# Narrow products between wide ones in two stages, and products of constants in a third

## The reference

```
x = x + 0.5 * swiglu(rmsnorm(x), ffn1)               # ffn
p = rmsnorm(x) @ w_in                                # mixer with convolution and delta rule
    y_a = gelu(u_a) * spatial_gating(gelu(v_a))
    qkv = silu(causal_dwconv(qkv)); q, k l2-normed
    beta = sigmoid(b_raw); g = -exp(a_log) * softplus(a_raw + dt_bias)   # 4 + 4 narrow columns of w_in
    o = gated_delta_rule(q, k, v, beta, g)           # chunks of 64 tokens
x = x + concat(y_a, rmsnorm(o) * silu(z)) @ w_out
x = x + 0.5 * swiglu(rmsnorm(x), ffn2);  x = rmsnorm(x, final_norm)
h = rmsnorm(x); q, k, v, og, f_logit, u = split(h @ hy_w_in)             # f_logit: 8 narrow columns
    cum = cumsum(log_sigmoid(f_logit + f_bias))      # the forgetting mixer's decay
    attn = softmax(q k^T * scale + c_i - c_j, causal) @ v * sigmoid(og)
x = x + concat(attn, pooled(u)) @ hy_w_out
x = x + swiglu(...)
x = x + rwkv7_time_mix(rmsnorm(x))                   # bonus = sum(r * k * r_k) per head, times v
x = x + swiglu(...)
```

## Time and profile before

| | us |
|---|---|
| median of 3 runs (1346.1 to 1346.85) | 1346.11 |
| the profiled execution | 1346.0 |
| its span in the profile | 1344.2 |
| PE busy / POOL / ACT / DVE | 1290.8 / 752.5 / 597.8 / 545.2 |

### The profile page before, as it was taken

How to read it: one execution, slowest core, us unless ns; L and a number is a source line. 1 busy time by engine, 2 the same in 40 slices (tenths; PEclk the granted TensorE clock), 3 DMA queues, 4 the chain that set the end, 5 groups by cost and what they waited for, 6 DMA issues and landing times.

```text
span 1344.2 us, 22609 instructions
## 1 busy us (share of the span) xinstructions
PE 1290.8 (96%) x9424; PEld 1130.2 (84%) x9424; DVE 545.2 (41%) x798; ACT 597.8 (44%) x773; POOL 752.5 (56%) x190
## 2 busy tenths in 40 slices
PE   6999999999999999897999999989998998999999
PEld 5888888888888888797698888867887997988887
DVE  4433334634333333437333333365847434333333
ACT  6444443224454444634455444434232334544442
POOL 2988850112478888565248888800034321698885
PEclk9999998999999999988899999989989997999999
DMA  6655552234255555444124555513441011455552
GB/s 260 211 195 188 187 198 94 94 106 177 96 179 197 187 187 187 151 155 157 63 78 173 192 191 194 196 71 130 152 156 67 3 34 34 166 209 188 187 190 91
DMA packets 30570, 200.74 MB, mean 149 GB/s; under 512 B 3488, under 2 KB 5408, under 8 KB 6688
## 3 DMA queue, kind: packets, MB, share of 16 engines
q1 hardware_dynamic: 27632, 195.39, 40.8%
q10 hardware_dynamic: 2864, 4.27, 1.0%
HBM read 197.55 MB, written 2.10 MB: 149 GB/s over the span
## 4 chain that ended last, share of the span: by engine, by line
PE 90%; DVE 5%; ACT 3%; issue 1%; DMA 0%; POOL 0%; SPq 0%; ACTq 0%; DVEq 0%
PE psum L326 24%; PE psum L328 12%; PE psum L317 9%; PE psum L319 8%; PE psum L318 8%; PE psum L911 7%; PE psum L922 5%; PE psum L2333 1%; PE psum L2425 1%; DVE arena L1709 1%; PE psum L2441 1%; PE psum L314 1%; PE psum L1801 1%; PE psum L1800 1%; PE psum L2455 1%
## 5 line engine op out<-in xcount | busy, mean ns | idle before, releaser
L2742 POOL TENSOR_TENSOR wlo<-raw,whi 128x2048 fp32r<-128x2048 f32 x154 | 714.1, 4641 | 458.9 <-ACT whi L287 439.4
L326 PE MATMUL psum<-f_both,whi 128*128 128x512 f32 x1408 | 493.7, 394 | 2.1 <-DVE arena L835 2.1
L287 ACT ACTIVATE whi<-raw 128x2048 fp32r<-128x2048 f32 x154 | 294.9, 1916 | 254.9 <-PE psum L328 171.0
L328 PE MATMUL psum<-f_both,wlo 128*128 128x256 f32 x1408 | 394.3, 280 | 0.0
L326 PEld LDWEIGHTS psum<-f_both,whi 128*128 128x128 f32 x1408 | 265.2, 188 | 61.3 <-issue 2.7
L328 PEld LDWEIGHTS psum<-f_both,wlo 128*128 128x128 f32 x1408 | 265.4, 189 | 1.5
L317 PE MATMUL psum<-whi,ahi 128*128 128x512 f32 x352 | 137.3, 390 | 0.0
L319 PE MATMUL psum<-whi,alo 128*128 128x512 f32 x352 | 137.0, 389 | 0.0
L318 PE MATMUL psum<-wlo,ahi 128*128 128x512 f32 x352 | 136.9, 389 | 0.0
L833 DVE TENSOR_TENSOR psum<-psum,arena 128x512 f32<-128x512 f32 x44 | 30.8, 700 | 236.6 <-ACT arena L769 236.4
L850 DVE TENSOR_TENSOR alo<-arena,ahi 128x512 fp32r<-128x512 f32 x44 | 100.4, 2283 | 31.8 <-ACT ahi L784 31.8
(11 more groups left out here) (366 smaller groups left out, 1565.0 us busy)
## 6 DMA issues: line engine op xcount, KB each, us to landing
raw<-stream SPq DMA_DIRECT2D x183, 1024.0 KB, 4.9
con<-consts SPq DMA_DIRECT2D x1, 1184.0 KB, 12.9
x<-x_in SPq DMA_DIRECT2D x1, 1024.0 KB, 5.0
kept_x<-x ACTq DMA_DIRECT2D x1, 1024.0 KB, 3.9
x<-kept_x ACTq DMA_DIRECT2D x1, 1024.0 KB, 4.9
out<-x SPq DMA_DIRECT2D x4, 256.0 KB, 2.0
arena<-gm_w_s ACTq DMA_DIRECT2D x1, 512.0 KB, 5.7
arena<-final_norm ACTq DMA_DIRECT2D x1, 512.0 KB, 3.9
```

The source lines that it names most:

```text
L287: nc.scalar.activation(whi[:, slot, :], raw[:, c % RAW, :], ACT.Copy).then_inc(high_made, 1)
L326: nc.tensor.matmul(psum[:, bank, :].rearrange("p (a n) -> p a n", a=2), whi[w], f_both[:, :, k, :], start=k == 0, stop=False, skip_group_c ...
L328: return nc.tensor.matmul(psum[:, bank, 0:TOK], wlo[w], f_hi[:, k, :], start=False, stop=k == KT - 1, skip_group_check=True)
L2742: nc.gpsimd.tensor_tensor(wlo[:, slot, :], raw[:, c % RAW, :], whi[:, slot, :].bitcast(F32), ALU.subtract)\
```

## The change

In mix1 the narrow chunk is no longer a projection of its own. `plain_columns` calls a function before each of its 16 matmuls, and for chunk 7 that function issues one of the narrow matmuls. In rwkv the 16 bonus matmuls go in the same way between the 16 matmuls of value chunk 10. In fox, five fp32 matmuls of constants (128 x 256, into bank 5, whose result nobody reads) are issued ahead of the narrow chunk, and one after its 12th, 24th and 36th product. Nothing else is moved or taken out, and the other engines' programs are the same.

```diff
+        def idle_products(count, bank):
+            for _ in range(count):
+                nc.tensor.matmul(psum[:, bank, 0:256], const("ident"), con[:, 0:256], start=True, stop=True)
...
         def plain_columns(slot, bank, h, wait=None, parts=range(4), between=None):
...
+                    if between:
+                        between(j, k)
                     mm = nc.tensor.matmul(psum[:, bank, j * 256:(j + 1) * 256], raw[:, slot, k * 256 + j * P:k * 256 + j * P + P],
                                           h[:, k, :], start=k == 0, stop=k == KT - 1)
...
-            project(eng, W_IN(12), plain_tokens, n=8, h=hs, wait=lambda k: eng.wait_ge(S["h_low"], 8 * n + k + 1))
-            project(eng, W_IN(7), plain_columns, h=hs)
+            c_narrow = CH[W_IN(12)]
+            plain_loaded(eng, c_narrow)
+            def narrow(m, k):
+                if m == 0:
+                    eng.wait_ge(S["h_low"], 8 * n + k + 1)
+                mm = nc.tensor.matmul(psum[:, proj_bank(W_IN(12)), m * 256:m * 256 + 8], hs[:, k, m * P:m * P + P],
+                                      raw[:, c_narrow % RAW, k * 256:k * 256 + 8], start=k == 0, stop=k == KT - 1)
+                if (m, k) == (1, KT - 1):
+                    mm.then_inc(chunk_used, 1)
+            project(eng, W_IN(7), plain_columns, h=hs, between=narrow)
...
-            project(eng, N(8), tokens_out, n=8)
+            idle_products(5, 5)
+            project(eng, N(8), tokens_out, n=8, between=lambda m, k: idle_products(1, 5) if k % 4 == 3 else None)
...
+            def bonus_sum(m, k):
+                if (m, k) == (0, 0):
+                    eng.wait_ge(s("rw_rk"), 8)
+                mm = nc.tensor.matmul(psum[:, 4, 16 * m + 2 * k:16 * m + 2 * k + 2], rk[:, k, m * P:(m + 1) * P],
+                                      const("same64")[:, 0:P:64], start=True, stop=True)
+                if (m, k) == (1, KT - 1):
+                    mm.then_inc(s("rw_bonus_sum"), 1)
             for j in range(4):
-                project(eng, RW(8 + j), plain_tokens, h=variant_x[1], wait=made(5) if j == 0 else None)
-                if j == 1:
...
+                project(eng, RW(8 + j), plain_tokens, h=variant_x[1], wait=made(5) if j == 0 else None,
+                        between=bonus_sum if j == 2 else None)
```

More of the change, by code:

```diff
@@ L349, in columns_out, with tokens_out @@
             return mm
-        def tokens_out(slot, bank, hi=hhi, lo=hlo, n=256, halves=(0, 1), order=range(KT), wait=None):
+        def idle_products(count, bank):
+            for _ in range(count):
+                nc.tensor.matmul(psum[:, bank, 0:256], const("ident"), con[:, 0:256], start=True, stop=True)
+        def tokens_out(slot, bank, hi=hhi, lo=hlo, n=256, halves=(0, 1), order=range(KT), wait=None, between=None):
             for m in halves:
@@ L360, in tokens_out @@
                                       False, k == order[0], k == order[-1])
+                    if between and (m, k) != (halves[-1], order[-1]):
+                        between(m, k)
             return mm
@@ L902, in plain_loaded, with plain_columns @@
             eng.wait_ge(raw_loaded[c % RAW], 16 * (c // RAW + 1))
-        def plain_columns(slot, bank, h, wait=None, parts=range(4)):
+        def plain_columns(slot, bank, h, wait=None, parts=range(4), between=None):
             for part in parts:
@@ L913, in plain_columns, with plain_tokens @@
             return mm
-        def plain_tokens(slot, bank, h, wait=None, n=256, parts=range(4)):
+        def plain_tokens(slot, bank, h, wait=None, n=256, parts=range(4), between=None):
             for part in parts:
@@ L2372, in rwkv_tensor @@
                     square_sums(3)
-            for j in range(4):
-                project(eng, RW(8 + j), plain_tokens, h=variant_x[1], wait=made(5) if j == 0 else None)
-                if j == 1:
[L2377 to L2382, removed]
+            def bonus_sum(m, k):
[5 more added lines that the diff above has]
+                    mm.then_inc(s("rw_bonus_sum"), 1)
+            for j in range(4):
+                project(eng, RW(8 + j), plain_tokens, h=variant_x[1], wait=made(5) if j == 0 else None,
+                        between=bonus_sum if j == 2 else None)
             def scores(m, i_, q):
```

## The result

| | before | changed |
|---|---|---|
| median of 5 runs each, us | 1346.54 (1346.1 to 1347.77) | 1354.13 (1353.77 to 1360.33) |
| the profiled execution / its span, us | 1346.0 / 1344.2 | 1353.77 / 1352.0 |
| PE busy, us | 1290.8 | 1294.3 |

The changed kernel is slower: ratio 1.0071, with an interval of 1.0054 to 1.0087. The difference of the medians is 7.6 us, that of the profiled executions 7.8 us.

The account below looks back on a forecast made before the run. PE was taken to bound the kernel, as the chain that ended last is PE for 90%. From 1346.0, +11.7 in mix1, -3.5 in rwkv and -0.6 in fox gave 1353.6 us; range 1344 to 1358.

Parts of the forecast that it names:

- The wait in mix1 and the fall in it: mix1: PE waits for bank 6 until 214.4, the clock falls, and 16 pairs at 1.28 us take until 234.7.
- Size of mix1: mix1: L1377 starts 10.4 us later, L1394 11.7 us later, and all of it carries to the end.
- the forecast wait of 1.2 us at the sums of squares: mix1: PE reaches L1394 at 243.8 and waits 1.2 us for the chain through chunk 7's convolution, ending at 245.0.
- rwkv: rwkv: pairs at 0.65 us keep the high clock; both chunks take 17.3 us instead of 20.9, -3.5 us.
- fox: fox: five constants cost nothing, the clock falls within the narrow chunk as late as in mix1; -0.6 us.
- Clock back soon in mix1: Rival, mix1: clock low for some 3.5 us, then pairs at 0.65; +3.9 us there, sum 1345.8; chance 0.28.
- Hidden weight loads: Rival, mix1 and rwkv: narrow weight loads hide under wide products, pair 0.43 us high; sum 1339.0; chance 0.06.
- High clock all through fox's chunk: Rival, fox: the clock never falls, -5.3 instead of -0.6; sum 1348.9 with the forecast's mix1; chance 0.08.
- No wait added: Rival, mix1: pairs start at 211.2 without a new wait, -1.0 us there; sum 1340.9; chance 0.03.

Follow-up runs that it names:

- the split version: Kernel before with rwkv as changed; in mix1 eight narrow products and three constants ahead of chunk 7's wait, eight between its first wide ones: 1343.24 us, ratio 0.9976.
- rwkv alone: Kernel before with only the rwkv bonus put between the matmuls of value chunk 10, mix1 and fox as before: 1343.5 us, ratio 0.9985.
- the wait alone: Kernel before with one wait moved: mix1's narrow chunk, still issued in one piece, also waits for bank 6: 1351.04 us, ratio 1.0033.

## Why the prediction was right

Forecast 1353.6 us, measured 1354.13, by the mechanism that it named. The terms were less exact than their sum, which came out so close by luck.

- **The wait in mix1 and the fall in it: right.** First narrow product at 214.5 (forecast 214.4), 1.28 us a pair, clock back only in the wide products behind. The kernel whose wait is cut to 0.9 us shows that without the wait the loss is gone; the one with the wait filled, that of the 12.7 us some 10 are the clock's and not the wait's; the one with the wait but no pairs (2.3 us late in its trace, 5.4 in the medians), that the pairs are what keeps the clock low for so long. The prediction read two rows loosely: PE did stop before the narrow products in mix1, for 0.3 us, and L1377 stood at 229.8 and not 229.7. Neither changes the argument.
- **Size of mix1: 12.7 instead of 11.7.** The prediction let the half of chunk 4 follow at once. It goes to bank 7, whose reader now comes after the pairs: 1.05 us of wait [before, the narrow chunk was read 17 us earlier, rows 3], and the products started at 236.4 instead of 234.7. In turn the forecast wait of 1.2 us at the sums of squares didn't appear, since PE was 2.1 us later there than forecast and ACT only 0.3.
- **rwkv: -3.4 for the two chunks, -3.5 forecast; -2.9 in the end.** This is the best founded of the terms, the same in seven traces. That the pairs keep the clock was read from mix1's levels and held. Not foreseen: it falls later, among the scores (1022.6), and that gives 0.5 us back.
- **fox: -0.6 within the chunk, as forecast, with the fall 3.4 us in.** In part luck: the four other traces of this chunk have the fall 2.5 or 5.5 us in, and 0.2 to 0.3 us more or 2.5 less than before. The stage behind it gave it back, as its own falls landed otherwise: the shift is 12.55 ahead of fox and 12.52 behind it.
- **Missing altogether:** -1.6 us at rwkv's start, where nothing is changed: the clock was low from 890.5 to 900.7 before and from 903.2 to 910 after. So 12.7 - 2.9 - 1.6 and -0.4 of small shifts give 7.8. Misses of +1.0, +0.6, +0.6 and -2.0 happened to cancel.
- **The rivals.** Clock back soon in mix1: false, 20 us at 0.50. The rule of the Trainium skill that stood beside it ("TensorE: Matmul & The Clock Gate", loop structure: matmuls without a wait between keep the clock up) agrees with the pairs of rwkv and of the kernel without the wait, which kept a high clock. It does not agree with narrow products alone, which lost it back to back, and the prediction's reading of it, that such a row also wins a low clock back, fails in mix1. Hidden weight loads: false, 0.66 us a pair. High clock all through fox's chunk: false, it fell 3.4 us in. No wait added: false; a changed DVE order (0.9 us of wait left) or the split version (0.3 us) come near it.

## What to carry to other kernels

When a narrow product is merged into a wide one's loop, it inherits every wait of the wide one, and its own reader and bank come free at the end of the merged loop: list both before the merge. Mixed narrow and wide products can hold a high clock, and yet not win back a low one; so see what PE does just before them, and fill a wait there rather than add one, best with work of the kernel's own.

## What the runs showed of the hardware that was not expected

The same pairs run at 0.50 for 20 us after a wait of 3.7 us (two traces), and at 1.00 for 10.4 us when PE was busy until 0.9 us before or throughout (all eleven other stretches of them, in eight traces). What the clock was at their start decided, not what they are.

The clock's falls land at other places from execution to execution, in code that no edit touches. Fox's attention had a low stretch of 10 us in 7 of the 14 traces and of 17 us in the other 7, 3.5 us apart in time. No edit is needed for it: two kernels whose fox code is the old one (rwkv alone, the wait alone) had the long one, and the first of them is the kernel before up to 990 us. The narrow chunk of fox, unchanged, took from 7.8 to 10.3 us in the same way. So part of the 8 us over which one kernel's runs spread is likely this, and a single trace can't price an edit to better than some us outside the stretch that it changes. Why the edit in fox alone measured slower, with its chunk 0.2 us longer in the trace, stays open, and so does what decides between 10 and 17 us: all seven long ones had a low stretch of 10 us some 17 us ahead of it, and six of the seven short ones had one of 7 there; the changed kernel had 10 and was short.
